# The experts' gate-up product with its operands exchanged: rows stationary on column halves and quarters, weights streaming

## The reference, cut to what matters

```python
gu = t[tok] @ w_gate_up[e] + b_gate_up[e]          # rows x 2048, gate and up columns alternate
gate = jnp.minimum(gu[:, 0::2], SWIGLU_LIMIT)
up = jnp.clip(gu[:, 1::2], -SWIGLU_LIMIT, SWIGLU_LIMIT)
act = (up + 1.0) * gate * jax.nn.sigmoid(SWIGLU_ALPHA * gate)
return act @ w_down[e] + b_down[e]
```

## Time and profile before

| | us |
|---|---|
| median of 3 runs | 3649.79 (3638.45 to 3654.53) |
| profiled execution | 3661.44, span 3659.8 |
| TensorE busy in the span | 3127.2 (85%) |
| VectorE, ScalarE busy | 1224.1, 601.5 |
| gate-up matmuls (L1587) on the chain that ended last | 32% of the span |
| down matmuls (L1598) on that chain | 18% |
| mean granted clock of TensorE | 0.915 of full speed |

### The profile page before, as it was taken

The page is one execution under the profiler, slowest core; times in us unless marked ns, Lnnn a source line. Parts: engine busy times, 40 slices in busy tenths (PEclk is TensorE's granted clock), DMA queues, the critical chain, the costliest instruction groups (busy, mean ns, idle before and its releaser), DMA issues.

```text
span 3659.8 us, 46853 instructions
## 1 busy us (share of the span) xinstructions
PE 3127.2 (85%) x15932; PEld 2365.5 (65%) x15933; DVE 1224.1 (33%) x3422; ACT 601.5 (16%) x1419; POOL 182.9 (5%) x188
## 2 busy tenths in 40 slices
PE   3577747999995997599999999998999998999991
PEld 1344426777772564487777777786777786777770
DVE  1145541666662554222222222222222221222224
ACT  0011110545551332011000010000111010000110
POOL 0000000000000011100000000000000000000000
PEclk8788865999997996799999999999999999999995
DMA  3521133233004110665544576565776674645735
GB/s 116 171 50 49 38 74 83 57 78 78 13 1 139 35 41 18 251 237 203 185 165 165 197 265 208 190 233 194 259 257 219 205 244 164 223 152 183 262 124 236
DMA packets 306054, 554.51 MB, mean 152 GB/s; under 512 B 80350, under 2 KB 115422, under 8 KB 304840
## 3 DMA queue, kind: packets, MB, share of 16 engines
q1 hardware_dynamic: 265912, 509.39, 41.2%
q0 software_dynamic: 21152, 38.50, 3.1%
q10 hardware_dynamic: 18832, 4.33, 0.5%
HBM read 525.89 MB, written 70.93 MB: 163 GB/s over the span
## 4 chain that ended last, share of the span: by engine, by line
PE 51%; issue 3%; DVE 2%; DMA 2%; ACT 1%; DVEq 1%; ACTq 0%; POOL 0%; POOLq 0%
PE ps L1587 32%; PE ps L1598 18%; DMA d_ys<-ys_e,dst 1%; PE ps L1570 1%; DVE x L1557 1%; ACT xT_e L1486 1%; DVE ys_e L1546 0%; DVE gg L1533 0%; DVEq L1402 0%; DMA xg<-d_h,src 0%; DVEq L1399 0%; ACTq L1405 0%; ACTq L1500 0%; ACT ss L1505 0%; DVE aT L1540 0%
## 5 line engine op out<-in xcount | busy, mean ns | idle before, releaser
L1587 PE MATMUL ps<-xT_e,wg 128*128 128x128 f32 (+2 forms) x8192 | 1274.8, 320 | 77.2 <-issue 40.4
L1587 PEld LDWEIGHTS ps<-xT_e,wg 128*128 128x128 f32 x8192 | 1233.1, 202 | 132.7 <-issue 57.9
L1598 PE MATMUL ps<-wd,aT 128*128 128x512 f32 x1504 | 650.8, 592 | 0.0
L1598 PEld LDWEIGHTS ps<-wd,aT 128*128 128x128 f32 x1504 | 283.5, 190 | 344.1 <-issue 344.1
L1533 DVE TENSOR_SCALAR gg<-ps,bias 128x128 f32<-128x128 f32 (+2 forms) x256 | 101.5, 396 | 792.7 <-PE ps L1587 792.5
L1546 DVE COPY ys_e<-ps 128x1024 f32<-128x1024 f32 x47 | 56.1, 1221 | 670.9 <-PE ps L1598 670.9
L1505 ACT ACTIVATE ss<-gg 128x128 f32<-128x128 f32 (+2 forms) x256 | 88.7, 346 | 962.3 <-DVE gg L1533 962.0
L428 PE MATMUL ps<-w_in,hT_a 128*128 128x430 f32 x512 | 187.6, 529 | 0.0
L1505 ACT ACT_TABLE_LOAD x32 | 41.1, 1283 | 879.8 <-issue 879.8
L777 ACT ACTIVATE sc<-sc,nm 128x640 f32<-128x640 f32 (+15 forms) x256 | 161.3, 633 | 70.1 <-DVE nm L810 70.1
L428 PEld LDWEIGHTS ps<-w_in,hT_a 128*128 128x128 f32 x512 | 98.2, 193 | 87.4 <-issue 87.0
(11 more groups left out here) (284 smaller groups left out, 2505.6 us busy)
## 6 DMA issues: line engine op xcount, KB each, us to landing
wg<-in_w_gate_up SPq DMA_DIRECT2D x128, 2048.0 KB, 8.0
wd<-in_w_down SPq DMA_DIRECT2D x128, 1024.0 KB, 4.9
wg<-d_ys SPq DMA_DIRECT2D x8, 2048.0 KB, 10.8
d_bias<-d_rev SPq DMA_DIRECT2D x1, 10368.0 KB, 39.6
w_in<-in_w_in SPq DMA_DIRECT2D x1, 6880.0 KB
x_a<-in_x POOLq DMA_DIRECT2D x8, 512.0 KB, 8.4
kn<-d_kn SPq DMA_DIRECT2D x8, 512.0 KB
strip_t<-d_bias SPq DMA_DIRECT2D x8, 512.0 KB
```

What stands on the lines that cost most here:

```text
L1587: mm = pe.matmul(ps[:, j % 2, half * PASS:half * PASS + w], wg[:, j // 2, k, c0:c0 + 255:2], xT[:, k, 0:w], start=(k == 0), stop=(k == KD ...
L1598: mm = pe.matmul(ps[:, 2 + 2 * b + h, :], aT[:, j, b * P:(b + 1) * P], wd[:, c, j % 2, h * 512:(h + 1) * 512], start=(j == 0), stop=(j == ...
```

## The change

Gate-up exchanges its operands: the transposed rows are stationary and 512 weight columns stream. A pass is cut into elements. A full element has 128 rows on all 128 array columns and one weight chunk; a half element has 64 rows placed twice, on array columns 0 to 63 and 64 to 127, each half with a chunk of its own; a quarter element has 32 rows placed four times with all four chunks. Six arms, chosen by the number of rows (64, 96, 128, 160, 192, 256), list their elements. The result has rows on the partitions and gate and up columns alternating, so the bias must lie on every partition: SP loads it for each expert as a 1 MB broadcast, between the gate-up and the down loads, and the setup's transposed biases go. VectorE adds it with one add per column part, then clamps and multiplies 256 columns at a time. The activated rows `aa` (rows on partitions) are turned back by two transposes per element on TensorE and copied into `aT` by ScalarE. An element's activation is turned after the next element's matmuls; the last one's after the second down chunk. `wd` is laid out so that two neighbouring hidden columns lie on one partition. Blocks with up to 64 rows use two column halves in the down product too (`half`). The next pass's row transposes are 8 instead of 16 if it has one block. VectorE's copies of the down result follow the blocks; `ys` is set to zero once instead of in each pass.

```diff
-CREDIT = 8
+CREDIT = 16
...
-        bgu = sb("bgu", [NE, 2 * FF])
-        ident = sb("ident_s", [P, P])
...
-                for half in range(2):
-                    for j in range(8):
-                        n = half * 8 + j
-                        mm = pe.transpose(ps[:, 4 + n // 4, (n % 4) * NE:(n % 4 + 1) * NE],
-                                          bgu[:, 2 * P * j + half:2 * P * (j + 1):2], ident[0:NE, 0:NE])
-                mm.then_inc(s_rows, 1)
...
+        CF = FF // NCH
+        FULL, HALF, QUARTER = P, P // 2, P // 4
...
-        bias = sb("bias", [P, 16])
-        gg, ss, uu = (sb(n, [P, 2, PASS]) for n in ("gg", "ss", "uu"))
+        bias = sb("bias", [P, 2 * FF])
+        gu, gg, ss, uu, vv = sb("gu", [P, 2 * CF]), sb("gg", [P, CF]), sb("ss", [P, CF]), sb("uu", [P, CF]), sb("vv", [P, CF])
+        aa = sb("aa", [P, 2, CF])
...
+        U = 8
+        W = 16
+        F0 = [(FULL, c, 0) for c in range(NCH)]
+        ARMS = {HALF: [(HALF, 0, 0), (HALF, 1, 0)],
+                HALF + QUARTER: [(QUARTER, 0, HALF), (HALF, 0, 0), (HALF, 1, 0)],
+                FULL: F0,
+                FULL + QUARTER: [(QUARTER, 0, FULL)] + F0,
+                FULL + HALF: [(HALF, 0, FULL), (HALF, 1, FULL)] + F0,
+                2 * FULL: [(FULL, c, b * P) for c in range(NCH) for b in range(2)]}
+        WEIGHTS_USED = {HALF: (8, 8), HALF + QUARTER: (1, 7, 8), FULL: (4, 4, 4, 4), FULL + QUARTER: (1, 3, 4, 4, 4),
+                        FULL + HALF: (1, 1, 2, 4, 4, 4), 2 * FULL: (2,) * 8}
...
+                            sp.wait_ge(s_gu, CREDIT + W * i + 4 * (c + 1) - W)
...
+                        sp.wait_ge(s_rd, CREDIT + U * i)
+                        hold(sp, e.sp_passed)
+                        sp.dma_start(bias[:, :], e.b_gate_up[0][one, :].rearrange("o n -> (o n)").partition_broadcast(P)).then_inc(s_bias, 16)
...
+                def copy_act(i, m, arm):
+                    kind, c, t0 = arm[m]
+                    act.wait_ge(s_aT, CREDIT + U * i + turned(m, arm))
+                    groups = P // kind
+                    out = aT[:, 2 * c * groups:2 * (c + 1) * groups, t0:t0 + kind].rearrange("p (g f) n -> p f g n", f=2)
+                    act.activation(out, ps[:, 6 + bank_of(m, arm), 0:2 * P].rearrange("p (f g n) -> p f g n", f=2, n=kind), ACT.Copy).then_inc(s_aTc, added(m, arm))
...
+                            def sigmoids(rows):
+                                arm = ARMS[rows]
+                                for m in range(len(arm)):
+                                    act.wait_ge(s_g, CREDIT + U * i + (U if last(m, arm) else m + 1))
+                                    act.activation(ss[:, :], gg[:, :], ACT.Sigmoid, scale=ALPHA).then_inc(s_sig, count(m, arm))
+                                    if m:
+                                        copy_act(i, m - 1, arm)
+                            by_rows(act, n, sigmoids)
+                            with act.If(after > P):
+                                copy_rows(i + 1, PASS)
+                            with act.Else():
+                                copy_rows(i + 1, P)
+                            def last_copy(rows):
+                                copy_act(i, len(ARMS[rows]) - 1, ARMS[rows])
+                            by_rows(act, n, last_copy)
...
+                        dve.wait_ge(s_bias, CREDIT + 16 * i + 16)
...
+                        def activate(rows):
+                            arm = ARMS[rows]
+                            used = 0
+                            for m, (kind, c, t0) in enumerate(arm):
+                                def wait(s):
+                                    dve.wait_ge(s, CREDIT + U * i + (U if last(m, arm) else m + 1))
+                                add = count(m, arm)
+                                used += WEIGHTS_USED[rows][m]
+                                groups = P // kind
+                                dve.wait_ge(s_gu, CREDIT + W * i + used)
+                                for g in range(groups):
+                                    part = slice(g * kind, (g + 1) * kind)
+                                    cols = slice((c * groups + g) * 512, (c * groups + g + 1) * 512)
+                                    read = dve.tensor_tensor(gu[part, :], ps[part, bank_of(m, arm), :], bias[part, cols], ALU.add)
+                                read.then_inc(s_rd, add)
+                                wait(s_rd)
+                                dve.tensor_scalar(gg[:, :], gu[:, 0::2], LIMIT, None, ALU.min).then_inc(s_g, add)
+                                dve.tensor_scalar(uu[:, :], gu[:, 1::2], LIMIT, -LIMIT, ALU.min, ALU.max).then_inc(s_u, add)
+                                wait(s_g)
+                                wait(s_u)
+                                dve.scalar_tensor_tensor(vv[:, :], uu[:, :], 1.0, gg[:, :], ALU.add, ALU.mult).then_inc(s_v, add)
+                                wait(s_v)
+                                wait(s_sig)
+                                dve.tensor_tensor(aa[:, bank_of(m, arm), :], vv[:, :], ss[:, :], ALU.mult).then_inc(s_a, add)
+                                if not last(m, arm):
+                                    wait(s_a)
+                        by_rows(dve, n, activate)
...
+                def turn_rows(i, nb, busy=None):
                     pe.wait_ge(s_x, 32 * i + 32)
                     for k in range(4):
                         pe.wait_ge(s_xTc, CREDIT + 4 * i + max(k - 1, 0))
+                        if k == 1 and busy is not None:
+                            pe.wait_ge(s_aTc, busy)
                         for kk in range(2):
+                            for b in range(nb):
                                 c = 2 * k + kk
+                                mm = pe.transpose(ps[:, 7 - k % 2, kk * PASS + b * P:kk * PASS + (b + 1) * P], xg[:, b, c * P:(c + 1) * P], ident[:, :])
                         mm.then_inc(s_xT, 1)
+                def turn_act(bank):
+                    for f in range(2):
+                        mm = pe.transpose(ps[:, 6 + bank, f * P:(f + 1) * P], aa[:, bank, f::2], ident[:, :])
+                    return mm
                 pe.wait_ge(s_id, CREDIT + 16)
+                turn_rows(0, 2)
                 with pe.Fori(0, NPASS) as i:
+                    n, after = rows_left(pe, i), rows_left(pe, i + 1)
                     with pe.If(n > 0):
+                        pe.wait_ge(s_xTc, CREDIT + 4 * i + 4)
+                        pe.wait_ge(s_rd, CREDIT + U * i)
+                        hold(pe, e.pe_passed)
+                        def gate_up(rows):
+                            arm = ARMS[rows]
+                            loaded = 0
+                            for m, (kind, c, t0) in enumerate(arm):
+                                groups = P // kind
+                                while loaded < (c + 1) * groups:
+                                    pe.wait_ge(s_wg[loaded], CREDIT + 16 * i + 16)
+                                    loaded += 1
+                                if m >= 2:
+                                    pe.wait_ge(s_rd, CREDIT + U * i + m - 1)
+                                for k in range(KD):
+                                    for g in range(groups):
+                                        mm = pe.matmul(ps[g * kind:(g + 1) * kind, bank_of(m, arm), :], xT[:, k, t0:t0 + kind], wg[:, c * groups + g, k, :],
                                                        start=(k == 0), stop=(k == KD - 1))
+                                mm.then_inc(s_gu, WEIGHTS_USED[rows][m])
+                                if m:
+                                    pe.wait_ge(s_a, CREDIT + U * i + m)
+                                    if m >= 3:
+                                        pe.wait_ge(s_aTc, CREDIT + U * i + m - 2)
+                                    turn_act(bank_of(m - 1, arm)).then_inc(s_aT, added(m - 1, arm))
+                            pe.wait_ge(s_aTc, CREDIT + U * i + len(arm) - 2)
+                            hold(pe, e.pe_passed)
+                        by_rows(pe, n, gate_up)
+                        with pe.If(after > P):
+                            turn_rows(i + 1, 2, CREDIT + U * i + U - 1)
+                        with pe.Else():
+                            turn_rows(i + 1, 1, CREDIT + U * i + U - 1)
+                        pe.wait_ge(s_aTc, CREDIT + U * i + U - 1)
+                        pe.wait_ge(s_y, CREDIT + 2 * i)
+                        hold(pe, e.pe_passed)
+                        def down(rows):
+                            def whole(b, c):
+                                for h in range(2):
+                                    for j in (2 * c, 2 * c + 1):
+                                        mm = pe.matmul(ps[:, 2 + 2 * b + h, :], aT[:, j, b * P:(b + 1) * P], wd[:, c, j % 2, h * 512:(h + 1) * 512],
+                                                       start=(j == 0), stop=(j == JD - 1))
+                                return mm
```

(67 more changed lines are left out.)

101 lines of the change are left out of this document (22 added, 79 removed).

## The result

The changed kernel takes 3720.2 us (median of 4, 3704.1 to 3725.0) where the kernel before takes 3649.9: the ratio is 1.019, with an interval of 1.015 to 1.0229. It is 1.9% slower; I had forecast 3474 us. The profiled execution, the shortest of the four, has a span of 3702.3 us.

The account below looks back on a forecast made before the run. TensorE's matmul stream was taken to bound the expert stage: passes 1811 us, branches 60, slow clock 10 and loads 10 make 1891 against 2067.6, so 3474 us for the kernel, range 3394 to 3595.

Parts of the forecast that it names:

- the number of long branches: TensorE's queue between passes and before down: about as many long branches as before, less hidden; 60 us, between 0 and 288.
- the second expert's loads: Weight and bias loads queued behind the first expert's would hold the second expert: 10 us, bounds 0 and 50.
- three in every pass: Rival: three long branches in every pass, +228 us, 3702 us, slower; chance 0.05.
- the 40.4 us: TensorE's waits with no releaser in the kernel before, taken as branches and as part of the stage's 82.6 us of waits.
- The clock: TensorE's clock is lower for a while after idle gaps: 10 us.
- The handover: Last gate-up matmul to first down matmul: 3.6 us for one block, 3.9 for two, 4.1 where the last element is half.
- The column splits: Gate-up and down: column halves and quarters run fully side by side, so a half or quarter element takes 6.9 us.
- The rivals that priced these at no or half overlap: Splits run one after the other: +571 us, 4045, chance 0.09; quarters overlap in pairs only: 3570, chance 0.12.
- By class: Whole passes by expert row count: 26.1 to 89.6 us each, summing to 1811 us against 1985 before.
- VectorE's branches: VectorE's new loop, some 450 instructions, would come close to missing its 512 resident; its branches took at most 69 ns before.
- The waits on VectorE's activation: TensorE's 36.8 us of waits inside gate-up go, the sigmoid coming with 4 us to spare.
- the sum: Expert stage: 1811 + 60 + 10 + 10 = 1891 us against 2067.6, a gain of 177 us.

Follow-up runs that it names:

- with shared code: Changed kernel, all six arms, but TensorE's code for the four full elements and for the two half elements written once, under conditions: 3485.9 us, ratio 0.9549.
- four arms: Changed kernel with only the arms for 96, 128, 160 and 256 rows, 96 KB of TensorE loop code: 3534.3 us, ratio 0.9687.
- dead code: Kernel keeping only arms 96, 128, 160, 256, plus TensorE code that no pass executes: 3842.9 us at 133 KB, 3608.1 at 115, 3528.8 at 106.
- 155 KB in stretches: Changed kernel, six arms, each arm's gate-up, turns and down laid together so TensorE chooses once per pass: 3581.1 us, ratio 0.9812.
- one bias load: Changed kernel, six arms, with the 1 MB bias broadcast loaded once before the loop instead of for each expert: 3711.7 us, ratio 1.0189.
- with two arms: Changed kernel with only the arms for 128 and 256 rows, no column splits in gate-up, down still on halves: 3669.2 us, ratio 1.0062.

## Why the prediction was wrong

**What failed: the number of long branches.** The step reads "I count about as many TensorE instructions as before (…), so I expect about as many long branches, but less hidden: 60 us". The count of instructions was right (a loop of 120 KB against 126), the conclusion was not. Before, a pass runs through one long body and one common part; after, its path goes through the arm, the transposes and one of four down products, in separate places. There are 57 long branches instead of 25. Idle time between passes is 181 us, 6 of them the second expert's loads. Ahead of down stand 5 more, 3.6 us each in the mean, in the passes of 97 to 128 rows; there the handover is 7.9 to 8.7 us instead of 3.6. The price of one branch was known from the earlier trace rows, and the rival "three in every pass", 3702 us, lies 18 us from the result. What it asked for came in part (two per pass in the mean, not three), and the rest of its price came from the clock; that its number is so near is luck. I gave it 0.05, because nothing in my argument made the count depend on how the code is laid out. Rows 8 had a hint: there one pass of before has three long branches in a row ahead of it and the next none, so it depended on the path. A smaller slip stands ahead of that step: 6.8 of the 40.4 us lie ahead of the first pass, outside the 2067.6, so the waits and the slow clock inside the stage were split wrongly by that much.

**The clock was mis-sized.** I gave it 10 us; it is up to 93, the difference between the measured and the undisturbed matmuls (58 in gate-up, 35 in down). Not all of it hangs on the branches: with shared code, where these are gone, the same difference is 60 us, of which 24 are waits on the activation. Some handovers cost clock too, also without a long branch: in the earlier trace rows 32 down records take 13.90 us, in the pass shown the first 16 take 8.82 and the next 7.13. It is not every handover: with shared code the granted clock is at its lower level in or just behind 14 of 32, and the undisturbed pass of two blocks has its handover of 4.2 us and a clock of 1.00.

**The handover was a little short.** Where nothing disturbs it, it takes 4.8 to 5.6 us for 65 to 96 rows (forecast 4.1) and 3.7 to 4.7 for more than 128 (forecast 3.9).

**What held.** The column splits overlap in full. A half element, 32 records, takes 7.09 us, and the quarter with its 64 records takes the other 7.0 of the 14.09 above; down on halves takes 3.65 us for 16 records. The rivals that priced these at no or half overlap are out. By class, the shortest passes of the kernel with shared code are 34.6, 41.4, 47.4, 61.0, 68.8 and 89.2 us against my 26.1, 40.1, 46.8, 61.2, 68.3 and 89.6; the first is long because so short a pass waits for GpSimd's gather of the next rows, 13.4 us in two passes, which I had not weighed. VectorE's branches stayed short (63 ns at most), and the loads held only the second expert, for 6.2 us.

**What held by luck.** The waits on VectorE's activation went from 36.8 us to 4.0, but I had argued that it comes with 4 us to spare, and with shared code it is up to 3.5 us late: the long branches hid it. And six arms with shared code take 3486 us, 12 from my number, which is no proof of the sum: that kernel has none of the 70 us that I gave to branches and loads, but 60 us instead of 10 of slow clock and waits on the activation, and about 30 us more of handover.

## What to carry to other kernels

Before giving a loop more arms, add up the code that each engine's loop spans and look at where the parts of one pass's path lie; long branches on an engine's queue in the trace of before were the sign here that residence was already incomplete, and the two arms more then cost some 6 us per pass. Write common parts once, under conditions, or put a whole path in one stretch. Price a gain from specialised arms together with the kernel that has fewer of them: four arms beat six here by 186 us with more work.

## What the runs showed of the hardware

- TensorE's code was fetched again from somewhere between 106 and 115 KB of loop on, in the kernels with four arms and dead code. A long branch took 2.7 to 7.7 us, and up to three came in a row (12.6 to 13.0 us of idle ahead of two passes in a row). 96 KB of code with 32 passes through four arms had one long branch.
- How much is fetched depends on the path: 155 KB in stretches had 29 long branches, 120 KB in scattered parts 57, the 126 KB of the kernel before 25.
- In fp32, two column halves and four column quarters of the array run fully beside each other: 7.0 us for 16 records of one full element, for 32 of a half one and for 64 of a quarter one.
- A 1 MB load that puts one row on all 128 partitions lands 11.1 us after its issue, behind 8 MB of weights on the same queue. The down loads behind it land after 8.7 us instead of 4.9, but they do so without it too (8.4 with one bias load), and with it and longer passes not (4.8 with two arms).
